# Hybrid conformer and state-space encoder on one core: weights and input of the next layer prepared inside the last phase, one wait placed later, and TensorE's four pairs written out

## What is computed

```python
proj = x @ w_in[i]          # one projection, cut into GLU, gates, z, xBC and dt
y_a = conformer_branch(...) # GLU, depthwise conv of 31 taps, LayerNorm, swish, matmul
y_b = mamba2_bidir_branch(...)  # conv of 5 taps, SiLU, chunked scan forward and backward, gated RMSNorm, matmul
merged = sigmoid(gate_a) * y_a + sigmoid(gate_b) * y_b
h  = layer_norm(ALPHA * x + merged @ w_o[i])
h2 = layer_norm(ALPHA * h + (silu(g_) * u_) @ w_down[i])   # g_, u_ = split(h @ w_gate_up[i])
x  = h2 + rms_norm(p[i] @ w_ple[i]) * sigmoid(h2 @ w_ple_gate[i])
```

## Time and profile before

| | us |
|---|---|
| median of 3 runs (2583.35, 2590.8, 2591.49) | 2590.8 |
| profiled execution, its own time | 2583.87 |
| its span | 2582.2 |
| TensorE matmuls busy | 2445.5 (95%) |
| VectorE busy | 1509.8 (58%) |
| ScalarE busy | 1317.2 (51%) |
| GpSimd busy | 614.6 (24%) |
| mean granted TensorE clock | 0.987 of full |

### The profile page before, as it was taken

The page is one execution under the profiler, slowest core; times in us unless marked ns, Lnnn a source line. Parts: engine busy times, 40 slices in busy tenths (PEclk is TensorE's granted clock), DMA queues, the critical chain, the costliest instruction groups (busy, mean ns, idle before and its releaser), DMA issues.

```text
span 2582.2 us, 34953 instructions
## 1 busy us (share of the span) xinstructions
PE 2445.5 (95%) x11436; PEld 1969.4 (76%) x11436; DVE 1509.8 (58%) x2555; ACT 1317.2 (51%) x1734; POOL 614.6 (24%) x733
## 2 busy tenths in 40 slices
PE   6999999899999999999879999999999999999997
PEld 5878778787877788887668787777878777888865
DVE  4799898988744311112548998899886433111125
ACT  4655545445564644345446455454555646443453
POOL 2424324133111011111024243241431111111110
PEclk8999999999999999999989999999999999999999
DMA  6467464655789588889355664747557885888893
GB/s 189 116 143 166 98 159 111 154 133 117 177 195 215 118 194 193 188 196 216 75 136 131 143 151 103 171 98 163 119 136 167 201 205 128 193 195 188 195 210 82
DMA packets 110420, 404.81 MB, mean 157 GB/s; under 512 B 12256, under 2 KB 12256, under 8 KB 109920
## 3 DMA queue, kind: packets, MB, share of 16 engines
q0 software_dynamic: 54144, 197.16, 44.7%
q1 hardware_dynamic: 55008, 201.61, 22.6%
q10 hardware_dynamic: 1152, 4.37, 0.5%
HBM read 400.99 MB, written 2.10 MB: 156 GB/s over the span
## 4 chain that ended last, share of the span: by engine, by line
PE 64%; DVE 16%; ACT 8%; issue 7%; DMA 3%; POOL 1%; ACTq 0%; DVEq 0%; SPq 0%; POOLq 0%
PE bank L729 18%; PE bank L731 18%; PE bank L730 18%; DVE tmp_m L1176 4%; ACT w_lo L434 2%; DMA w_raw<-w_stream 2%; DVE tmp_m L1172 2%; DMA w_lo<-w_stream 2%; ACT w_hi L433 2%; DVE xs_b_c L1094 2%; PE bank L771 1%; PE bank L772 1%; PE bank L774 1%; PE bank L868 1%; DVE y_tok L1203 1%
## 5 line engine op out<-in xcount | busy, mean ns | idle before, releaser
L729 PE MATMUL bank<-x_hi,w_hi 128*128 128x512 f32 x1856 | 741.4, 399 | 34.6 <-issue 19.8
L730 PE MATMUL bank<-x_lo,w_hi 128*128 128x512 f32 x1856 | 727.9, 392 | 0.0
L731 PE MATMUL bank<-x_hi,w_lo 128*128 128x512 f32 x1856 | 727.6, 392 | 0.0
L326 POOL DMA_DIRECT2D w_lo<-w_stream x376 | 327.2, 876 | 1646.2 <-ACT w_lo L434 1583.7
L433 ACT ACTIVATE w_hi<-w_raw 128x1024 fp32r<-128x1024 f32 x376 | 396.1, 1053 | 307.8 <-PE bank L731 242.9
L729 PEld LDWEIGHTS bank<-x_hi,w_hi 128*128 128x128 f32 x1856 | 351.4, 189 | 113.0 <-issue 34.4
L730 PEld LDWEIGHTS bank<-x_lo,w_hi 128*128 128x128 f32 x1856 | 351.9, 190 | 83.0 <-issue 10.7
L731 PEld LDWEIGHTS bank<-x_hi,w_lo 128*128 128x128 f32 x1856 | 351.5, 189 | 74.7
L434 ACT ACTIVATE w_lo<-w_raw 128x1024 fp32r<-128x1024 f32 x376 | 393.5, 1047 | 0.0
L1094 DVE SCALAR_TENSOR_TENSOR z_a<-glu_out,conv_a_params,z_a 128x497 f32 (+14 forms) x480 | 320.6, 749 | 0.0
L1456 DVE TENSOR_TENSOR glu_out<-bank,sigmoids 128x512 f32<-128x512 f32 x44 | 30.4, 692 | 414.1 <-PE bank L731 414.1
(11 more groups left out here) (212 smaller groups left out, 3641.2 us busy)
## 6 DMA issues: line engine op xcount, KB each, us to landing
w_raw<-w_stream SPq DMA_DIRECT2D x376, 512.0 KB, 4.5
w_lo<-w_stream POOLq DMA_DIRECT2D x376, 512.0 KB, 7.3
z_b<-x_in SPq DMA_DIRECT2D x4, 512.0 KB, 6.1
w_ple_in<-w_ple ACTq DMA_DIRECT2D x2, 1024.0 KB, 9.7
out<-z_b SPq DMA_DIRECT2D x1, 2048.0 KB, 6.3
ple_p<-p_in ACTq DMA_DIRECT2D x2, 512.0 KB, 5.3
params<-par_in ACTq DMA_DIRECT2D x2, 340.0 KB, 3.0
tmp_m<-w_dt ACTq DMA_DIRECT2D x2, 256.0 KB, 4.9
```

The lines of the kernel that those rows point to most:

```text
L326: gp.dma_start(wlo[:, s, :], w_stream[cyc, s].bitcast(F32R), accum_op=ALU.add).then_inc(lo_done[s], 16)
L729: pe.matmul(dst, wh, mh, start=first, stop=False)
L730: pe.matmul(dst, wh, ml, start=False, stop=False)
L731: return pe.matmul(dst, wl, mh, start=False, stop=last)
```

## The change

Nothing is computed differently. Work is moved:

- In the last phase of a layer ScalarE rounds the new x as its tiles come (`next_x`), and splits the next layer's first two weight tiles behind the sigmoids of the second cycle. VectorE makes `x_lo` of a tile behind the sum of the next one (`rest_of_x`). So that `x_hi` and `x_lo` are free, the last LayerNorm writes its rounded output to `act_a_hi` and `act_a_lo`, and the last phase reads these. Ahead of the first layer the same steps stand once by themselves.
- The parameters' load stands first in ScalarE's layer, which for layer 0 is behind the first two splits.
- In the first pair TensorE's `cumulative` comes after the third `dense` tile (before: after the second), and ScalarE's exponentials (`decays`) ahead of the read-out of the fourth tile (before: ahead of that of the first). For this ScalarE's first pair is written out and the other three are looped.
- SyncE loads two tiles more at the end, copies of the stream's first two, which ScalarE splits and nobody uses.
- TensorE's four pairs are written out. The loop over the layers stays.

```diff
@@ SyncE
+            tile(ALL_CYCLES, 0)
+            tile(ALL_CYCLES, 1)
             sp.wait_ge(xn_ready, seen((LAYERS + 1) * KT))
             sp.dma_start(out, zb[:, :, :]).then_inc(out_stored, 16)
@@ ScalarE
-            def norm_round(k, m, z, off):
+            def norm_round(k, m, z, dst, off):
...
+            def decays(L):
+                act.wait_ge(cum_done, seen(L + 1))
+                act.activation(stepf[:, WDEC:DOUT + 1, :], halves(bank[5]), ACT.Exp).then_inc(cum_exp, 1)
+                act.activation(stepf[:, TOT, :], bank[6][:, 0:GW], ACT.Exp).then_inc(cum_exp, 1)
+
+            def pair(L, base, j, first=False):
...
+                for c in range(4):
+                    if first and c == 3:
+                        decays(L)
+                    conv_input(G0, c, c0, c)
...
             act.wait_ge(consts, CONSTS)
+            for m in range(KT):
+                if m % 2 == 0:
+                    act.wait_ge(x_loaded[m // 2], 16)
+                act.activation(xh[:, m, :], zb[:, m, :], ACT.Copy).then_inc(xh_done, 1)
+            hi((0, 0), 0, 1)
             settle(act)
             with act.Fori(0, LAYERS) as L:
                 base = (L * CYCLES, L * BANK_CYCLES)
+                act.dma_start(par[:, :], par_in[L]).then_inc(par_loaded, 16)
                 want(4, ACT.Exp)
-                act.wait_ge(used[3], seen(base[1]))
-                for m in range(KT):
...
-                    act.activation(xh[:, m, :], zb[:, m, :], ACT.Copy).then_inc(xh_done, 1)
-                act.dma_start(par[:, :], par_in[L]).then_inc(par_loaded, 16)
-                hi(base, 0, 1)
                 act.wait_ge(dt_done, seen(2 * L + 1))
...
-                act.wait_ge(cum_done, seen(L + 1))
-                act.activation(stepf[:, WDEC:DOUT + 1, :], halves(bank[5]), ACT.Exp).then_inc(cum_exp, 1)
-                act.activation(stepf[:, TOT, :], bank[6][:, 0:GW], ACT.Exp).then_inc(cum_exp, 1)
-                with act.Fori(0, PAIRS) as j:
...
+                pair(L, base, 0, True)
+                with act.Fori(1, PAIRS) as j:
+                    pair(L, base, j)
...
+                def next_x(m):
+                    act.wait_ge(xn_ready, seen(KT * (L + 1) + m + 1))
+                    act.activation(xh[:, m, :], zb[:, m, :], ACT.Copy).then_inc(xh_done, 1)
+
                 for i in range(KT // SLOTS):
                     for s in range(SLOTS):
                         act.wait_ge(pg_used, seen(KT * L + SLOTS * i + s))
                         take(on(post, C_PLE + i), s, sg[:, :], ACT.Sigmoid)
                         if i == 0:
                             hi(on(post, C_PLE + 1), s)
+                        elif s < 2:
+                            hi((base[0] + CYCLES, base[1] + BANK_CYCLES), s)
+                        if i or s:
+                            next_x(SLOTS * i + s - 1)
+                next_x(KT - 1)
@@ TensorE
                 dense(c0, 0, xh, xl)
                 dense(c0, 1, xh, xl)
+                dense(c0, 2, xh, xl)
                 if first:
                     cumulative(L)
-                dense(c0, 2, xh, xl)
                 dense(c0, 3, xh, xl)
...
-                pair(L, base, 0, True)
-                with pe.Fori(1, PAIRS) as j:
-                    pair(L, base, j)
+                for j in range(PAIRS):
+                    pair(L, base, j, j == 0)
...
-                phase(post, C_PLE, CYCLES, xh, xl, ready=...)
+                phase(post, C_PLE, CYCLES, aah, aal, ready=...)
@@ VectorE
+            def rest_of_x(layer, m):
+                dve.wait_ge(xh_done, seen(KT * layer + m + 1))
+                rest(xl[:, m, :], zb[:, m, :], xh[:, m, :], xl_done)
+
+            for m in range(KT):
+                rest_of_x(0, m)
...
-                for m in range(KT):
-                    dve.wait_ge(xh_done, seen(KT * L + m + 1))
-                    rest(xl[:, m, :], zb[:, m, :], xh[:, m, :], xl_done)
...
-                norm_apply(NORMS * L + LN_2, zb, xh, xl, xl_done, O_LN2)
+                norm_apply(NORMS * L + LN_2, zb, aah, aal, xl_done, O_LN2)
...
                                              in1=ge[:, m, :], op0=ALU.add, op1=ALU.add).then_inc(xn_ready, 1)
+                    if m > 0:
+                        rest_of_x(L + 1, m - 1)
+                rest_of_x(L + 1, KT - 1)
```

More of the change, by code:

```diff
@@ new lines, in pair @@
+            def pair(L, base, j, first=False):
+                c0 = (base[0] + j * PAIR_CYCLES, base[1] + j * PAIR_BANKS)
+                G0 = L * GROUPS + j * 2
+                G1 = G0 + 1
+                act.wait_ge(conv_done, seen(4 * G0))
+                for c in range(4):
+                    if first and c == 3:
+                        decays(L)
+                    conv_input(G0, c, c0, c)
+                z_gates(G0, on(c0, 1), (0, 1))
+                silu(G0, 0)
+                silu(G0, 1)
+                act.wait_ge(conv_done, seen(4 * G0 + 2))
+                conv_input(G1, 0, on(c0, 1), 2)
+                xs_tokens(G0, 0)
+                xs_tokens(G0, 1)
+                silu(G0, 2)
+                silu(G0, 3)
+                decay(G0, 0)
+                conv_input(G1, 1, on(c0, 1), 3)
+                decay(G0, 1)
+                b_tokens(G0)
+                act.wait_ge(conv_done, seen(4 * G0 + 4))
+                conv_input(G1, 2, on(c0, 2), 0)
+                decay(G0, 2)
+                state(G0, 0)
+                silu(G1, 0)
+                silu(G1, 1)
+                conv_input(G1, 3, on(c0, 2), 1)
+                decay(G0, 3)
+                state(G0, 1)
+                state(G0, 2)
+                for c in range(CH):
+                    square(G0, c)
+                z_gates(G1, on(c0, 2), (2, 3))
+                decay(G1, 0)
+                want(2, ACT.Silu)
+                xs_tokens(G1, 0)
+                xs_tokens(G1, 1)
+                round_y(0, G0, 0)
+                round_y(0, G0, 1)
+                silu(G1, 2)
+                silu(G1, 3)
+                b_tokens(G1)
+                hi(on(c0, 4), 0)
+                take(on(c0, 3), 1, sg[:, :], ACT.Sigmoid)
+                decay(G1, 1)
+                state(G1, 0)
+                state(G1, 1)
+                decay(G1, 2)
+                state(G1, 2)
+                hi(on(c0, 4), 1)
+                decay(G1, 3)
+                want(3, ACT.Sigmoid)
+                hi(on(c0, 4), 2)
+                act.wait_ge(evac[0], seen(c0[1] + 4))
+                take(on(c0, 3), 3, sg[:, :], ACT.Sigmoid)
+                hi(on(c0, 4), 3)
+                for c in range(CH):
+                    square(G1, c)
+                round_y(1, G1, 0)
+                round_y(1, G1, 1)
+                for s in range(SLOTS):
+                    act.wait_ge(used[1 + s % 2 * 2], seen(c0[1] + 5 + s // 2))
+                    hi((c0[0] + 5, c0[1] + 4), s)
@@ L667, in _ @@
                 for m in range(KT):
-                    norm_round(k, m, za, O_LN1)
+                    norm_round(k, m, za, xh, O_LN1)
                     if m + 2 < KT:
@@ L706, in _ @@
                 for m in range(KT):
-                    norm_round(k, m, zb, O_LN2)
+                    norm_round(k, m, zb, aah, O_LN2)
                 act.wait_ge(esq_used, seen(L + 1))
@@ L1031, in _ @@
                 e_mean_square(range(4, KT))
-                phase(post, C_PLE, CYCLES, xh, xl, ready=lambda m: pe.wait_ge(xl_done, seen(KT * (k + 2) + m + 1)))
+                phase(post, C_PLE, CYCLES, aah, aal, ready=lambda m: pe.wait_ge(xl_done, seen(KT * (k + 2) + m + 1)))
         @block.vector
@@ L1584, in layout @@
         "p_in": p[:, 0].transpose(0, 2, 1).reshape(LAYERS, 2, P, T).transpose(0, 2, 1, 3),
-        "w_stream": np.stack(stream).reshape(ALL_CYCLES, SLOTS, P, WT),
+        "w_stream": np.stack(stream + stream[:SLOTS]).reshape(ALL_CYCLES + 1, SLOTS, P, WT),
         "w_dt": np.stack(w_dt + w_dt[:1]),
```

5 lines of the change are left out of this document (1 added, 4 removed).

## The result

The kernel after takes 2544.9 us, the median of 6 runs (2544.43 to 2552.37), against 2591.1 (2583.35 to 2593.77) before: 46 us less, a ratio of 0.9831 (95% interval 0.9815 to 0.9848). The profiled execution is one of 2544.5 us with a span of 2541.8, so the two profiled spans differ by 40.4 us.

The account below looks back on a forecast made before the run. TensorE, with 64% of the chain of waits, was taken to bound the kernel. 9.7 + 11.1 + 7.4 - 0.3 + 16.0 = 43.9 us gave 2540 or 2547; 2545 was chosen, range 2532 to 2561.

Parts of the forecast that it names:

- dt and the layer's jump: Layer 1's start, last phase's end to first dense tile: 9.7 us gained, with TensorE's own layer jump charged at 3.4.
- the forecast's sign: Before layer 1's first dt matmul: TensorE idle for 2 to 4 us, marked "issue".
- First pair of layer 1: Layer 1's pair 0, first dense matmul to L785: 11.1 us of wait and slow clock go; lower end 4.
- tight dates: Layer 1's first pair: two of four checked dates, slot 2's and slot 1's DMA, met with a few tenths to spare.
- Softplus: Layer 1's first pair: softplus takes 10.94 us, from about 1299.5 to 1310.5, before cumulative is wanted at 1313.4.
- Layer 0: Layer 0's start to L785: 7.4 us gained from the wait and half the slow clock, less 0.3 for the parameters' load.
- The loop: TensorE's loop over pairs: four jumps back cost 16.0 us, which writing the pairs out saves; ends 12.7 and 16.0.
- the trace bears out the warning: Loop over pairs: jumps outside two pages stall on a fetch, against a 2048-instruction store that would make the term 0.
- The written-out program stalls as well: Rival: TensorE's straight code also stalls on instruction fetches, so the 16.0 us do not come: 2561; chance 8%.
- slower: Rival: instruction fetch falls behind in TensorE's straight code, 36 packets stalling 1.87 us each: 2630; chance 3%.
- The start is bound anew: Rival: slot 2 or slot 1 lands late, or the layer jump costs 5.7; half of 28 us returns: 2559; 12%.
- Covers: Last phase: VectorE's rests and ScalarE's rounding and splits fit into mostly idle or covered slots, costed at nothing.

Follow-up runs that it names:

- sums-early kernel: Kernel after, with running sums again behind the second dense tile and exponentials again ahead of the first read-out: 2564.19 us, ratio 0.9893.
- padded kernels: Kernel after with TensorE's pairs 1 to 3 looped again, plus 16, 32, 64 or 160 semaphore increments ahead: 2577.06, 2545.07, 2546.61, 2561.7 us.
- written-out-only kernel: Kernel before, with TensorE's four pairs written out and nothing else: 2575.33 us, ratio 0.9934.
- kernel with the splits at the start: Kernel after, with the layer's first two weight tiles split at its start, the rounding of x left in the last phase: 2561.49 us, ratio 0.988.
- one with x late: Kernel after, with rounding of the next x and its rest all behind the last sigmoid, first two tiles still split early: 2547.19 us, ratio 0.9833.

## Why the prediction was right, and where it was not

The mechanism was right: every part of the gain came where it was forecast. That the median of 2544.9 meets the 2545 is in part luck. The sum of 43.9 us, taken from the profiled execution, gave 2540, and the profiled execution after took 2544.5: the parts gave 44.4, and 4 were lost elsewhere. Taken from the median it gave 2547, and the median fell by 46.2, since the profiled execution of before lay 7 us below its median and that of after does not. 2545 was chosen between the two, and so their errors cancelled.

- **dt and the layer's jump** (9.7 forecast, 12.0 measured). The jump was charged at 3.4 us and cost none, so the forecast's sign of 2 to 4 us marked "issue" before the first dt matmul did not come. Instead ScalarE's jump, which the text set down only as part of the parameters' date, stands ahead of the read-out of dt with its table load: 1.84 us, where 0.77 had been taken. In the other kernels whose dt matmuls find x ready the gap there was 0 to 1.8 us, so 3.4 was too much. What sets it stays open: the sums-early kernel has as many TensorE instructions as the kernel after and shows 1.54 us where that has none, in one execution each.
- **First pair of layer 1** (11.1, measured 10.7). Both tight dates held: no wait before the third dense tile and none before z_tiles. The sums-early kernel shows the price where the second does not.
- **Softplus.** The forecast date held, with the sums in their later place: softplus ends at 1300.70 and the sums start at 1302.01. It took 12.0 us, where 10.94 had been taken.
- **Layer 0** (7.1, measured 5.7). The first dense tile came 0.46 us later, of the forecast's kind (0.3), and the stretch was 43.8 instead of 42.5. The forecast let half of 3.8 us of slow clock go; 43.78 less 39.50 and 1.1 leaves 3.2, so nearly all of it stayed.
- **The loop** (16.0, measured 16.0). The size was right; the reading of it was not whole. The step "all instructions are the same, so the jumps cost" this made it a price of looping, and "the trace bears out the warning" set the figure of 2048 aside. The padded kernels bear out the figure: with 32, 64 and 160 increments the body is held and the jump is free. They go against the warning as it is worded, since these jumps go back over some 1600 instructions, far more than two pages of 256, without a stall. What made the jumps dear before is the place where the loop begins, which neither sentence of the Trainium skill gives.
- **Rivals.** "The written-out program stalls as well" and "slower" fell with the written-out-only kernel: no new gap over 0.4 us. "The start is bound anew" did not come either.
- **Covers.** Sigmoids, sums and the output were not held up by the work put behind them, as forecast: TensorE has no gap over 0.4 us in the last phase beyond the 3.55 at its head, which was there before. But the phase is 1.0 to 1.1 us longer in each layer, which the forecast had at nothing. The last section tells more.

## What to carry to other kernels

A gap marked "issue" behind a loop's jump can be a fetch of instructions: count the instruction packets of a straight and of a looping stretch, and before writing a loop out try the same loop a few dozen instructions further on; this body of some 1600 instructions is free in one place and costs 3.4 to 8.1 us a jump in another. Such a place also shifts with any edit ahead of it, so a timing of an unrelated edit can hold 16 or 30 us of it. At a boundary between phases look for the longest hand-over (here split, DMA, first matmul) and start that one early; and when the start moves forward, move what waits for a fixed chain (here softplus) back by the same.

## What the runs showed of the hardware that was not expected

The jump's cost ran from 0 to 8.1 us with 16 instructions' shift (stretches of 59.23 to 67.36 us), as above.

TensorE's matmuls of the `dense` shape follow each other every 227 ns at full clock where they read `x_hi` and `x_lo`, and every 233 ns where they read `act_a_hi`, `act_b_hi` or `y_hi` with their `lo`, in the kernel before as well. The change moved the last phase from the first to the second, and its 192 matmuls take 1.1 us more. The phase is 47.0 us in the three kernels that read x there and 48.1 to 48.2 in the other eleven. The kernel with the splits at the start has neither the splits nor their DMA in it (DMA share 0.38, as before) and the one with x late not the roundings, and both are as long as the rest, so the covered work is not the cause. Why the pace differs by tile stays open.

An increment of a semaphore on TensorE's queue costs about 0.15 us: with 64 and 160 in a row the first matmul came at 14.88 and at 29.55 us, 14.67 later for 96 more. The 0.13 that the expectation for 32 used had part of them hidden in the wait for x.

One VectorE instruction of the softplus chain takes 4.18 us in layer 1, where the same line takes 0.29 in layer 0. Timelines of VectorE and GpSimd in the kernel after:

```profile
1291.71 4.18 DVE L1330 TENSOR_SCALAR decay<-decay 128x256 f32<-128x256 f32 x1
...
1291.78 3.86 POOL L391 MEMSET z_b<- 128x4096 f32 x1
```

It ends 0.25 us behind GpSimd's clearing of z_b. In the earlier trace rows's chain the same happens to another TENSOR_SCALAR. The clearing meets the chain at a different place in every kernel, 28 times in the 14 profiled executions. Each time the TENSOR_SCALAR that runs when the clearing ends is over 0.15 to 0.25 us later, having taken 0.9 to 4.2 us, while each SCALAR_TENSOR_TENSOR beside the clearing takes its usual 0.43. That the clearing holds it rests on these; no kernel without the clearing was run.
